# A four-layer decoder trunk on one core: both mixers' product orders joined, remainders on GpSimd, the last norm's mean in two products

## The reference

```
for i in (0, 1):
    x = LN(alpha*x + 0.5*swiglu(x))                 # FFN, 2816 hidden
    x = LN(alpha*x + (swa, nsa)[i](x))              # the mixer
    x = LN(alpha*x + cross_attention(x, mem))       # 4 heads, 256 memory tokens
    x = LN(alpha*x + 0.5*swiglu(x))
```

## Time and profile before

| what | value |
|---|---|
| median of three runs | 2330.74 us (2329.08 to 2331.08) |
| the profiled execution | 2335.74 us, span 2333.5 us |
| mean granted clock of PE | 0.989 |
| busy: PE, DVE, ACT, POOL | 97%, 32%, 36%, 48% of the span |
| DMA | 204.92 MB, 88 GB/s on average |

### The profile page before, as it was taken

The page is one execution under the profiler, slowest core; times in us unless marked ns, Lnnn a source line. Parts: engine busy times, 40 slices in busy tenths (PEclk is TensorE's granted clock), DMA queues, the critical chain, the costliest instruction groups (busy, mean ns, idle before and its releaser), DMA issues.

```text
span 2333.5 us, 27961 instructions
## 1 busy us (share of the span) xinstructions
PE 2258.2 (97%) x10928; PEld 1855.0 (79%) x10928; DVE 736.2 (32%) x1498; ACT 840.4 (36%) x1433; POOL 1114.2 (48%) x693
## 2 busy tenths in 40 slices
PE   9999999889999999999999999989989999999998
PEld 7888888667888888888888888776667888888886
DVE  2111126555535111114211112645653535111115
ACT  3322233553435322223422223445653434322223
POOL 5454445446446544444644444434446545444443
PEclk9999999999999999999999999999999999999999
DMA  5332324212413333333333232210003313333331
GB/s 184 99 100 91 99 83 126 64 37 91 131 51 100 108 99 96 95 95 96 98 100 99 90 100 91 85 52 19 19 19 100 118 37 91 108 98 90 101 94 60
DMA packets 57874, 204.92 MB, mean 88 GB/s; under 512 B 6928, under 2 KB 7056, under 8 KB 57232
## 3 DMA queue, kind: packets, MB, share of 16 engines
q1 hardware_dynamic: 56016, 197.68, 28.3%
q10 hardware_dynamic: 1728, 5.45, 0.7%
HBM read 201.01 MB, written 2.10 MB: 87 GB/s over the span
## 4 chain that ended last, share of the span: by engine, by line
PE 90%; DVE 3%; ACT 2%; POOL 2%; issue 2%; DMA 0%; ACTq 0%; DVEq 0%
PE bank L1301 24%; PE bank L1302 24%; PE bank L1303 24%; PE bank L1604 2%; POOL w_lo L458 2%; PE bank L1327 2%; PE bank L1334 1%; PE bank L1565 1%; PE bank L1321 1%; PE bank L1537 1%; PE bank L1377 1%; PE bank L1379 1%; PE bank L1378 1%; PE bank L1538 1%; ACT w_hi L617 1%
## 5 line engine op out<-in xcount | busy, mean ns | idle before, releaser
L458 POOL TENSOR_TENSOR w_lo<-w_raw,w_hi 128x1024 fp32r<-128x1024 f32 (+1 forms) x374 | 888.5, 2379 | 950.6 <-ACT w_hi L617 950.2
L1301 PE MATMUL bank<-x_hi,w_hi 128*128 128x512 f32 x1520 | 595.8, 392 | 15.8 <-DVE h_lo L1108 12.6
L1302 PE MATMUL bank<-x_lo,w_hi 128*128 128x512 f32 x1520 | 593.2, 390 | 0.0
L1303 PE MATMUL bank<-x_hi,w_lo 128*128 128x512 f32 x1520 | 593.1, 390 | 0.0
L617 ACT ACTIVATE w_hi<-w_raw 128x1024 fp32r<-128x1024 f32 (+1 forms) x379 | 391.3, 1036 | 530.8 <-PE bank L1303 492.5
L1301 PE MATMUL bank<-h_hi,w_hi 128*128 128x512 f32 x960 | 379.9, 396 | 3.4 <-POOL w_lo L458 2.5
L1302 PE MATMUL bank<-h_lo,w_hi 128*128 128x512 f32 x960 | 374.5, 390 | 0.0
L1303 PE MATMUL bank<-h_hi,w_lo 128*128 128x512 f32 x960 | 374.4, 390 | 0.0
L1301 PEld LDWEIGHTS bank<-x_hi,w_hi 128*128 128x128 f32 x1520 | 286.3, 188 | 73.9 <-DVE h_lo L1108 13.4
L1303 PEld LDWEIGHTS bank<-x_hi,w_lo 128*128 128x128 f32 x1520 | 286.0, 188 | 60.1
L1302 PEld LDWEIGHTS bank<-x_lo,w_hi 128*128 128x128 f32 x1520 | 286.5, 188 | 56.2
(11 more groups left out here) (218 smaller groups left out, 2576.0 us busy)
## 6 DMA issues: line engine op xcount, KB each, us to landing
w_raw<-w_dram SPq DMA_DIRECT2D x315, 512.0 KB, 3.6
w_raw<-w_dram SPq DMA_DIRECT2D x64, 448.0 KB, 3.3
f<-mem_dram ACTq DMA_DIRECT2D x3, 1024.0 KB, 5.0
out_dram<-t SPq DMA_DIRECT2D x8, 256.0 KB, 2.1
t<-x_dram SPq DMA_DIRECT2D x2, 512.0 KB, 6.8
f<-cmp_w_dram ACTq DMA_DIRECT2D x1, 1024.0 KB, 8.2
t<-x_dram ACTq DMA_DIRECT2D x2, 256.0 KB, 5.4
t<-x_dram ACTq DMA_DIRECT2D x1, 512.0 KB, 8.1
```

What stands on the lines that cost most here:

```text
L458: pool.tensor_tensor(w_lo[:, slot(s), 0:n * P], w_raw[:, s % RAW, 0:n * P], w_hi[:, slot(s), 0:n * P].bitcast(F32), ALU.subtract).then_inc ...
L1301: pe.matmul(dst, w_hi[:, slot(s), w], m_hi[:, k, :], start=k == 0, stop=False)
L1302: pe.matmul(dst, w_hi[:, slot(s), w], m_lo[:, k, :], start=False, stop=False)
L1303: last = pe.matmul(dst, w_lo[:, slot(s), w], m_hi[:, k, :], start=False, stop=k == n - 1)
```

## The change

- **Starts.** SWA and the cross attentions no longer use `together`: the first slab runs by itself in `alone` (eight hi-hi products, eight with w_lo, eight with x_lo), then two slabs by `product`. `together` stays in the FFNs and NSA, and now ends slab by slab.
- **SWA's table.** Chunks of the next query slab stand in units 0 to 3 of a pair, two in each (they stood from one unit before to unit 3); `q_done` is unit 3 (it was 4).
- **Last pairs of both mixers.** Six chunks of the first output slab stand in the last pair (`within`); `early` has 15 chunks left instead of 21 and puts one ahead of the values and one behind.
- **NSA's head.** Token tiles 0 and 1 stay ahead of unit 0; the others follow the scores of units 1 and 3 (`TOKENS`). The tiles are taken from the last one down, the gates are formed tile by tile (`gate`), q1's chunks stand in units 5 to 12 (they were 1 to 8), and its `q_done` is 14 (10). The feeds of vs, vw, q1, q2 and q3 move.
- **Fills.** `by_dve` holds only slab 0: POOL makes all remainders. In stages 1 and 5 `FILL_BEHIND` sets behind which x_hi chunks ACT feeds and copies: 1 and 4, and 3 and 6, instead of 1, 3 and 5 with a first feed behind chunk 0.
- **`out_bases`.** POOL makes a weight remainder behind base 2 and behind each base from 4 on (before: behind 2 and then behind 7).
- **Last norm.** The mean is the sum of two products, of the first seven chunks' sum and of chunk 7; ACT copies it at once; DVE centres chunks 0 to 2, two of them between the small steps, POOL 3 to 7.

```diff
-LAST = (4, 5, 6, 7)
+LAST = (3, 4, 5, 6, 7)
+FILL_BEHIND = {1: (1, 4), 5: (3, 6)}
+TOKENS = {1: 2, 3: 3}
...
-        self.early = [(j, k) for k in range(KC - 1) for j in range(2)] + [(2, k) for k in range(KC - 1)]
+        self.within = [(0, k) for k in range(KC - 2)]
+        self.early = [(1, k) for k in range(KC - 2)] + [(j, KC - 2) for j in range(2)] + [(2, k) for k in range(KC - 1)]
...
+        self.within = [self.base[7] + (1 + k if kind == "swa" else 2 + 2 * k) for k in range(6)]
...
-                at = max(b - 1 + k * 5 // 8, 0) if self.kind == "swa" else b + 1 + (k if p == 0 else 3 * k // 2)
+                at = b + k // 2 if self.kind == "swa" else b + (5 + k if p == 0 else 1 + 3 * k // 2)
...
-            if n == self.base[p] + (4 if self.kind == "swa" else 10 if p == 0 else 13):
+            if n == self.base[p] + (3 if self.kind == "swa" else 14 if p == 0 else 13):
...
-                    if j == 2:
-                        feed(first + 3)
-                feed(first + 7)
+                    if j == 2 or j >= 4:
+                        feed(first + max(j, 3))
...
-                    if j == 0:
+                    if j == 0 and st.ln not in FILL_BEHIND:
                         ahead(1)
-                    if j in (1, 3, 5):
-                        m = (j + 1) // 2
+                    after = FILL_BEHIND.get(st.ln, (1, 3, 5))
+                    if j in after:
+                        m = after.index(j) + 1
+                        ahead(m)
                         fill(m + 1)
-                        if m >= 2:
-                            ahead(m)
...
-                    if len(st.fill) == 5 and j in (1, 3, 5) and st.by_dve[j // 2 + 2]:
-                        remainder(st.fill[j // 2 + 2][2][1])
...
+            def alone(st, s, dst):
+
+                pe.wait_ge(hi_ready, s + 1)
+                for k in range(KC):
+                    pe.wait_ge(xhi_ready, KC * st.ln + k + 1)
+                    pe.matmul(dst, w_hi[:, slot(s), k * P:(k + 1) * P], x_hi[:, k, :], start=k == 0, stop=False)
+                wait_lo(pe, s)
+                for k in range(KC):
+                    pe.matmul(dst, w_lo[:, slot(s), k * P:(k + 1) * P], x_hi[:, k, :], start=False, stop=False)
+                for k in range(KC):
+                    pe.wait_ge(x_ready, KC * st.ln + k + 1)
+                    last = pe.matmul(dst, w_hi[:, slot(s), k * P:(k + 1) * P], x_lo[:, k, :], start=False,
+                                     stop=k == KC - 1)
+                last.then_inc(slab_done, 1)
...
-                    together(st, [(sl["ks0"], bank[2][:]), (sl["ks1"], bank[3][:]), (sl["q0"], bank[4][:])])
+                    alone(st, sl["ks0"], bank[2][:])
+                    product(sl["ks1"], bank[3][:], x_hi, x_lo, KC)
+                    product(sl["q0"], bank[4][:], x_hi, x_lo, KC)
...
+                    tokens(st, 1)
                     pe.wait_ge(z["clo"], 1)
                     pe.wait_ge(z["chi"], 5)
                 for n in range(M.end):
                     if n < M.n:
                         scores(st, M, M.units[n])
+                    if st.kind == "nsa" and n in TOKENS:
+                        tokens(st, TOKENS[n])
                     for p, k in M.q_chunks(n):
                         q_chunk(st, M, p, k)
+                    if n in M.within:
+                        if n == M.within[0]:
+                            pe.wait_ge(z["qlo"], 16)
+                        for j, k in st.within[:1]:
+                            out_slab(st, 0, j, range(k, k + 1))
+                        st.within = st.within[1:]
...
+                if st is final:
+                    total = dtotal
+                    pe.wait_ge(dsum_ready, 7 * st.ln + 6)
+                    pe.matmul(bank[B_MEAN][:], ones[:], dsum, start=True, stop=False)
+                    pe.wait_ge(dev, KC * (st.ln + 1))
+                    pe.matmul(bank[B_MEAN][:], ones[:], t[:, KC - 1, :], start=False, stop=True).then_inc(mean_rep, 1)
...
+                if st is final:
+                    dve.wait_ge(mean_here, 1)
+                    centre(0)
                 dve.wait_ge(sq_tok, st.ln + 1)
                 dve.wait_ge(msq_ready, st.ln + 1)
                 dve.tensor_tensor(var4, bank[B_VAR][:, 0:4], msq4, ALU.subtract).then_inc(stat, 1)
+                if st is final:
+                    centre(1)
```

More of the change, by code:

```diff
@@ L213, in plan @@
     fills = 0
-    by_dve = [0]
     for ln in range(NLN):
@@ L1313, in together @@
                 behind = 2
[L1314 removed]
+                for k in range(KC):
                     w = slice(k * P, (k + 1) * P)
[L1316 to L1321 removed]
+                    pe.wait_ge(xhi_ready, KC * st.ln + k + 1)
+                    for s, dst in group:
+                        if k == 0:
+                            pe.wait_ge(hi_ready, s + 1)
+                        pe.matmul(dst, w_hi[:, slot(s), w], x_hi[:, k, :], start=k == 0, stop=False)
+                    if k == KC - 1:
+                        break
                     for s, dst in group:
@@ L1662, in mixer, with tokens @@
                             values(st, M, v)
-                    if n == M.n:
-                        pe.wait_ge(z["add"], M.n)
                     if n >= M.n:
-                        early(st, 2)
-                early(st, 21)
+                        early(st, 1)
+                early(st, 15)
                 out(st, 0, {0: 7, 1: 7, 2: 7})
+            def tokens(st, k):
+                sl = st.slab
+                last = token_major([sl["vs"], sl["vw"], sl["gl"]], bank[(7, 0, 1, 2)[k]][:, 0:384], NT - 1 - k, x_hi, x_lo,
+                                   384)
+                if k == NT - 1:
+                    last.then_inc(slab_done, 3)
+                else:
+                    last.then_inc(st.sem["post"], 1)
             def early(st, count):
@@ L1678, in cross @@
                 z, sl = st.sem, st.slab
-                together(st, [(sl["q0"], bank[2][:]), (sl["q1"], bank[3][:]), (sl["q2"], bank[4][:])])
+                alone(st, sl["q0"], bank[2][:])
+                product(sl["q1"], bank[3][:], x_hi, x_lo, KC)
+                product(sl["q2"], bank[4][:], x_hi, x_lo, KC)
                 fill_banks(st)
```

146 lines of the change are left out of this document (79 added, 67 removed).

## The result

The changed kernel takes **2305.8 us** (median of 4 runs, 2303.9 to 2308.1); the kernel before, measured beside it, 2330.9 (2329.1 to 2332.2). The ratio is 0.9893 with a 95% interval of 0.9876 to 0.9910: faster by 25 us. Forecast were 2301 us and a range of 2286 to 2315. The profiled execution took 2303.9 us with a span of 2302.1; it is the fastest of its four, and the one of before, 2335.7, lay 5.0 above its median. So the two spans are 31.4 us apart and the medians 25.1.

What follows compares the result with a forecast made beforehand. TensorE, busy 97% of the span, was taken as the bound, leaving only its idle and slow-clock time to win. Terms summed to 30.1 us: 2305.6 for the profiled execution, less 5.0 for the median, 2301 us; range 2286 to 2315.

Steps and rivals of the forecast that it cites:

- SWA's start: First slab of SWA: v1's remainder is ready in time, removing a 3.3 us wait and 1.4 of slow clock; -4.7 us.
- SWA's pairs: Steady pairs: six waits for the query's `h_lo` go, 0.9 us each stays, a slow stretch probably goes; -8.7 us.
- SWA's last pair and end: Six output chunks fill waits for `pf` and spare slow clock, but are missing at the end (+1.5); -3.0 us.
- NSA's first pair: Waits of 3.1 and 2.7 us and 3.2 of slow clock go, 2.0 remains; -7.0 us.
- NSA's last pair and end: The same six chunks: 2.0 us of waits filled, 2.0 of new wait at the end; 0, ends -2 and +2.
- NSA's output product: Remainders between POOL's bases remove a 2.51 us wait and the 1.3 us slow stretch behind it; -3.8 us.
- fills, cross 1: Ahead of the first cross attention: waits and slow clock go, but a later feed costs +2.6; -2.4 us.
- fills, cross 2: Ahead of the second cross attention: 1.8 and 1.1 us go, but a later feed costs +4.2; +1.3 us.
- locked out: Rival: each of four remainders moved to POOL delays a DVE x_lo by 1.5 us at cross attentions; 2307 us, chance 0.08.
- `alone` starves: Rival: at three starts PE waits for the last x_hi, up to 14.5 us each; 2344 us, chance 0.02.
- Chains hold: Rival: DVE's and ACT's chains per unit set the mixers' pace, SWA's pairs give only 1.5 us; 2315 us, chance 0.15.
- all covered: Rival: no wait stays in SWA's pairs, none appears at mixer ends, feeds come in time; 2285 us, chance 0.12.

Runs made afterwards that it cites:

- e3: Changed kernel with NSA's old head: all four token tiles and gates ahead of the pairs, q1's chunks in units 1 to 8; 2314.3 us, ratio 0.9942.
- e5: Changed kernel with the old last pairs: no output chunks within them, 21 left for `early`, two behind each step's values; 2313.0 us, ratio 0.9925.
- e7: Changed kernel with GpSimd's five bases in a row again, remainders behind base 2 and then only base 7, in all four output products; 2317.9 us, ratio 0.9948.
- e2: Changed kernel with `together` back in place of `alone` and two products at SWA's start only; 2305.4 us, ratio 0.9900.
- e1: Changed kernel with SWA's old places of the query chunks and of `q_done`, the last pair's six chunks kept; 2318.6 us, ratio 0.9954.
- f1: Kernel before with only the new order of GpSimd's bases and remainders, in all four output products; 2326.9 us, ratio 0.9985.
- e6: Kernel of e4 with DVE again making two weight remainders in each of stages 1 and 5; 2310.7 us, ratio 0.9917.
- e4: Changed kernel with `FILL_BEHIND` empty, so ACT's old feed places return while GpSimd still makes all remainders; 2302.5 us, ratio 0.9891.
- b2: Changed kernel with ACT's old fill feeds, `alone`'s last two chunks apart, and DVE's rest of SWA's query slab in halves; 2290.4 us, ratio 0.9828.
- b3: Changed kernel with old fill feeds, `alone`'s last two chunks apart, q3's remainder behind the compressed unit, three chunks kept for mixer ends; 2291.1 us, ratio 0.9829.

## Why the prediction held, and where it did not

Where a part was taken back alone, its worth is the growth at its place; otherwise it is read between the two traces.

| term | forecast | measured |
|---|---|---|
| SWA's start | -4.7 | -2.2 between the traces, -0.6 in e3, e5 and e7, whose start is the same; 0 for `alone` by e2 |
| SWA's pairs | -8.7 | -9.2 (e1) |
| SWA's last pair and end | -3.0 | -2.4 (e5) |
| NSA's first pair | -7.0 | -7.4 (e3) |
| NSA's last pair and end | 0 | -1.5 (e5) |
| NSA's output product | -3.8 | -3.5 (f1), -5.1 (e7) |
| SWA's output product | none | 0 alone (f1), -4.9 beside the other parts (e7) |
| fills, cross 1 | -2.4 | -0.4 |
| fills, cross 2 | +1.3 | +2.6 |
| last norm | -1.6 | -2.1 |

With SWA's start at 2.2 us and the bases at f1's 3.5 these come to about 26 us, beside 25 between the medians; with e7's 10.0 they come to 33, since the bases then count what they are worth only beside the other parts. The fills of cross 1 and the last norm were not taken back alone.

**SWA's start failed.** The step was that the last two x_hi are written from 394.10 to 395.50 and PE begins at 394.2. Both moved. PE began at 392.20, since the fills ran with one pause of 0.24; and x_hi's last chunk, 1.3 us sooner on the clock if nothing had changed, came at 396.46. The rows of before were taken for the time of a chunk that the change itself delays: ACT now feeds a group's slabs ahead of its copy, in this stage too, and POOL's two remainders (5.17 us from 391.62) lie over an x_lo of 2.49 us; that the feed's place put them there was not tested.

```profile
391.62 5.17 POOL L461 TENSOR_TENSOR w_lo<-w_raw,w_hi 128x1024 fp32r<-128x1024 f32 x2 [1.38 <-ACT w_hi L621]
392.08 2.49 DVE L1049 SCALAR_TENSOR_TENSOR x_lo<-t,lnb,x_hi 128x512 fp32r<-128x512 f32 x1
396.46 0.72 ACT L729 ACTIVATE x_hi<-t,lnb 128x512 fp32r<-128x512 f32 x1 [2.88 <-DVE t L1043]
```

The first score is 3.48 us sooner (427.09 before, 423.61 now), of which 1.3 come from ahead of the stage. So "locked out" and "`alone` starves" were both real, at this place together, for 3.1 us. As cases for the whole they fell: e6 shows that moving remainders from DVE to POOL gains 6 us in spite of the lock, and PE waited for x_hi at one start of three (at two in e4).

**SWA's pairs held.** Forecast were 12.2 us a pair and 0.9 of wait; it is 12.54 in the mean, with two waits, 0.66 for the score behind the query's rest and 0.48 for `pf`:

```profile
433.15 0.48 PE L1591 MATMUL bank<-mv,h_lo 128*128 128x128 f32 x1 [2.24 <-DVE small L1247]
457.99 0.33 PE L1591 MATMUL bank<-mv,h_lo 128*128 128x128 f32 x1 [0.66 <-DVE small L1247]
470.54 0.33 PE L1591 MATMUL bank<-mv,h_lo 128*128 128x128 f32 x1 [0.66 <-DVE small L1247]
```

The first of the two was missed, and so was the first pair's wait of 2.24 us (the row at 433.15): the list of DVE's work was laid against the values, not against unit 4's bias, which stands behind both halves. b2 shows that this one was free to take. "Chains hold" (1.5 us for the pairs) is out by e1, and "all covered" (no wait left) by the same rows.

**NSA's head held**, term by term: 3.1 and 2.7 us of waits went, and of the 2.0 that were kept for the compressed unit and the rest one wait of 2.06 was left. The reason given, a DVE instruction stretched by POOL's remainder, was the right one in kind; the one that counted was the TENSOR_SCALAR at L1198 beside q3's remainder (b3), not the subtraction beside q2's.

**The last pairs** were right: 2.4 us in SWA for 3.0, and 1.5 in NSA for a term of 0 with ends of 2 either way. In NSA 2.0 filled against 2.0 of new wait was right as idle time (the end waits 1.41 us for `h_lo`); what was not in the sum is that the long wait of 2.06 us in e5 is followed by 3.4 us at half clock and the short ones are not. **The output products** had the right mechanism for NSA in the kernel as it was; that SWA's would have needed the same edit once the other parts are in was not seen, since the edit was priced only at the wait of the trace before. It does not show in the total, because both edits came together.

**The fills** were forecast 2.0 and 1.3 us too kindly. Cross 1 was given one wait of 2.6 and got two, of 0.84 and 2.90, and a slow stretch behind it; cross 2 had 4.2 and got 4.88 and a stretch of 6.8 us at half clock:

```profile
1791.60:1798.40 6.80, 4.82 (x22) 4.85 (x23) 6.73 (x10) 3.72 (x5) 3.09 (x2) 0.50 0.50 154
```

The place (feed behind x_hi's chunk 3) and the mechanism were as forecast; e4 takes the wait away.

**The last norm** held: from DVE's last chunk (2317.45 before, 2288.14 now) to the end it was 16.05 us and is 13.96.

**From spans to medians** is where the 4.8 us between 2301 and 2305.8 lie. The terms come to 30.1 and the spans differ by 31.4, but by compensation: SWA's window gave 4.6 us less than its terms (11.8 against 16.4), cross 1 and 2 gave 2.0 and 1.3 less, NSA gave 7.4 more (18.4 against 0.2 + 7.0 + 0 + 3.8 = 11.0), the start 1.3 and the last norm 0.5 more. Read in steps of half a microsecond, the clock in before's trace is at half for thirteen times 3.4 us, and in the changed kernel's for five times (without the last norm's end): at 1.7 us each that is 13.6 of the 31.4 us. NSA's surplus is mostly such stretches in before's profile that no edit touched; f1, whose NSA differs from before's by one wait of 2.5, has 7.8 us less of busy time there. Such stretches come and go between executions, and are the likely reason why before's profiled run lay 5.0 above its median. The step from 2305.6 to 2301 took a profiled run's bad luck for something that stays the same distance from the median after the change; the changed kernel's profiled run lay 1.9 below its own. The medians moved by 25, and that the spans moved by nearly the forecast 30.1 is in part luck.

## What to carry to other kernels

A wait moved to another place is priced with the traces of the old order only until the same change moves what ends it: for each new wait, list what the edits do to the engine that ends it as well as to the one that waits. An edit that is worth little alone may be what another needs (the bases: 3.5 us alone, 10 to 13 beside the other parts), so parts are to be taken back from the joined kernel, not only tried on the old one. When a part's worth is read from one trace, count from its own first wait, and look for slow stretches that lie where nothing moved: here they made up 1.3 to 1.6 us in windows that grew by 3.0 to 10.8. And of idle time, break up the long waits first: in e5 the two long waits had slow stretches behind them, and the filled last pairs, with nearly the same idle time, had none.
